# Rows of both moving operands 160 bytes from the weights' place within 256 bytes, where they were 192

## What is computed

```python
hn = rmsnorm(h, norm_mix_g)
proj = hn @ w_in + b_in                       # q, k, v, gates, convolution inputs
y_m = mlstm_and_gate(proj) @ w_branch_m
y_c = (cb * causal_dwconv(cc * ch, conv_w)) @ w_branch_c
h = h + (sigmoid(gm) * y_m + sigmoid(gc) * y_c) @ w_out
hn = rmsnorm(h, norm_ffn_g)
gate, val = split(causal_dwconv(hn @ w_up, ffn_conv_w, ffn_conv_b))
h = h + (silu(gate) * val) @ w_down
```

## The kernel before

| tensor | address before | within 256 | place before |
|---|---|---|---|
| whi, wlo | 49280, 65664 | 128 | |
| hn, from its 64th value, high and low | 98624 + 256 | 64 | 192 |
| act, high and low | 135488 | 64 | 192 |
| hn, from its 48th value (272 columns) | 98624 + 192 | 0 | 128 |
| lo2, row 0, 1, 2, 3 and so on | 208672 + 1088 a row | 32, 96, 160, 224 | 160, 224, 32, 96 |

## Time and profile before

### The profile page before, as it was taken

One profiled execution on the slowest core, in us unless ns is written; L12 is line 12 of the kernel. 1 busy time (PEld: TensorE's weight loads), 2 busy tenths in 40 slices (PEclk: granted clock), 3 DMA queues, 4 the chain that ended last, 5 costly groups with the idle time before them and its releaser, 6 DMA issues.

```text
span 2870.7 us, 53265 instructions
## 1 busy us (share of the span) xinstructions
PE 2744.2 (96%) x22994; PEld 2721.2 (95%) x22994; DVE 1711.4 (60%) x1725; ACT 1300.1 (45%) x1449; POOL 1.8 (0%) x14
## 2 busy tenths in 40 slices
PE   4988999999999999999999967999999999999998
PEld 4987999999999999999989967999999999999998
DVE  4544565566667567657785648755665555455555
ACT  3443454444554355445544375444454334343443
POOL 0000000000000000000000000000000000000000
PEclk9988999999999999999999988999999999999999
DMA  4442555555555555555545424555556565655653
GB/s 154 162 146 93 195 193 192 190 191 191 187 194 180 197 182 196 198 191 165 173 165 171 154 98 132 191 185 182 190 179 189 189 182 187 191 183 185 186 183 115
DMA packets 257814, 503.17 MB, mean 175 GB/s; under 512 B 10150, under 2 KB 19038, under 8 KB 257630
## 3 DMA queue, kind: packets, MB, share of 16 engines
q1 hardware_dynamic: 254592, 500.20, 53.1%
q10 hardware_dynamic: 3054, 0.55, 0.1%
HBM read 498.63 MB, written 2.10 MB: 174 GB/s over the span
## 4 chain that ended last, share of the span: by engine, by line
PE 87%; DVE 7%; ACT 4%; ACTq 1%; issue 1%; DVEq 0%
PE psum L461 27%; PE psum L462 27%; PE psum L463 26%; PE psum L485 2%; PE psum L486 2%; PE psum L487 2%; DVE wlo L1040 2%; DVE work L1068 1%; DVE work L1408 1%; ACT whi L727 1%; ACTq L713 1%; DVE misc L1454 0%; ACT misc L950 0%; DVE hn L1078 0%; DVE work L1439 0%
## 5 line engine op out<-in xcount | busy, mean ns | idle before, releaser
L1040 DVE TENSOR_TENSOR wlo<-raw,whi 128x1024 fp32r<-128x1024 f32 x952 | 1160.1, 1223 | 983.6 <-ACT whi L727 982.7
L727 ACT ACTIVATE whi<-raw 128x1024 fp32r<-128x1024 f32 x952 | 1003.3, 1058 | 1317.4 <-PE psum L463 1194.3
L461 PE MATMUL psum<-hn,whi 128*128 128x256 f32 x4448 | 1249.5, 281 | 38.9 <-DVE wlo L1040 25.9
L462 PE MATMUL psum<-hn,whi 128*128 128x256 f32 x4448 | 1247.0, 280 | 0.0
L463 PE MATMUL psum<-hn,wlo 128*128 128x256 f32 x4448 | 1246.7, 280 | 0.0
L461 PEld LDWEIGHTS psum<-hn,whi 128*128 128x128 f32 x4448 | 846.1, 190 | 42.6 <-DVE wlo L1040 28.9
L463 PEld LDWEIGHTS psum<-hn,wlo 128*128 128x128 f32 x4448 | 848.7, 191 | 0.0
L462 PEld LDWEIGHTS psum<-hn,whi 128*128 128x128 f32 x4448 | 842.5, 189 | 0.1
L461 PE MATMUL psum<-act,whi 128*128 128x256 f32 x2544 | 711.8, 280 | 14.8 <-DVE wlo L1040 9.3
L463 PE MATMUL psum<-act,wlo 128*128 128x256 f32 x2544 | 711.0, 279 | 0.0
L462 PE MATMUL psum<-act,whi 128*128 128x256 f32 x2544 | 710.9, 279 | 0.0
(11 more groups left out here) (207 smaller groups left out, 978.3 us busy)
## 6 DMA issues: line engine op xcount, KB each, us to landing
raw<-in_w_in SPq DMA_DIRECT2D x160, 1024.0 KB, 5.1
raw<-in_mlp_w SPq DMA_DIRECT2D x128, 1024.0 KB, 5.3
raw<-in_w_up SPq DMA_DIRECT2D x80, 1024.0 KB, 5.0
raw<-in_w_down SPq DMA_DIRECT2D x40, 1024.0 KB, 5.1
raw<-in_w_out SPq DMA_DIRECT2D x32, 1024.0 KB, 5.0
raw<-in_w_branch_m SPq DMA_DIRECT2D x8, 1024.0 KB, 5.0
raw<-in_w_branch_c SPq DMA_DIRECT2D x8, 1024.0 KB, 5.0
raw<-in_w_up SPq DMA_DIRECT2D x8, 768.0 KB, 4.4
```

The costliest lines, as they stand in the source:

```text
L461: mm(o, hi[:, kk, w], both[:, 0, :], start=first, stop=False)
L462: mm(o, hi[:, kk, w], both[:, 1, :], start=False, stop=False)
L727: A(whi[:, n % SLOTS, :], raw[:, n // 2 % RAW, n % 2 * HALF:(n % 2 + 1) * HALF], ACT.Copy)\
L1040: V.tensor_tensor(wlo[:, n % SLOTS, :], raw[:, n // 2 % RAW, n % 2 * HALF:(n % 2 + 1) * HALF], whi[:, n % SLOTS, :].bitcast(F32), ALU.subt ...
```

## The change

`gap_a` has 40 values where it had 48. All that is declared behind it lies 32 bytes lower.

```diff
-        sb("gap_a", [P, 48])
+        sb("gap_a", [P, 40])
         hn = sb("hn", [P, NT, MAIN + 2 * T], F32R)
         act = sb("act", [P, NT, 2 * T], F32R)
```

## The result

The changed kernel takes 2931.86 us, the median of four runs (2910.89 to 2938.26), against 2865.29 us before. The ratio on record is 1.022 with a 95% interval from 1.0166 to 1.0273; the quotient of the two medians, 1.023, lies inside it. It is slower by 2.2%, where 2923 us in a range from 2835 to 2942 was forecast. A fifth run, outside the median, took 2922.67 us.

What follows compares the result with a forecast made beforehand. TensorE's distance between matmul starts was taken as the bound. The profiled 2872.45 us plus 51 us for 256-column matmuls, between 38 and 64, with other parts at zero, gave 2923 us, range 2835 to 2942.

Steps and rivals of the forecast that it cites:

- VectorE and ScalarE at other places: Both engines' reads and writes at shifted addresses: priced at zero, with slack as cover.
- Transfers: Transfers into raw, whose address stays: nothing priced.
- The 272-column groups: 1536 matmuls of 272 columns at shifted addresses: at most 2 us either way, taken as nothing.
- The price of place 160: 20976 matmuls of 256 columns, moving rows at 160 instead of 192 bytes (within 256) from the weights: plus 51 us.
- the lower bound: 256-column matmuls: only the 113.35 ns distance is forbidden, all go at 117.7 ns, loss 38 us.
- the middle that was chosen: 256-column matmuls: 51 us, taken between losses of 38 and 64 us.
- the upper bound: 256-column matmuls: 106.7 ns plus the 12.3 ns extra of 272-column matmuls, 119.0 ns, loss 64 us.
- the short pattern: Stretches of 256-column matmuls 113.35 ns apart, 8725 of them before, against 117.7 ns in the others.
- What would show it: Signs: one distance near 118 to 119 ns, none at 113.3, half clock at 213, idle before L461 not growing.
- Only the draw changes: At TensorE's restarts only the pattern fallen into changes; 2868 us, 10 us either way; chance 0.22.
- Place 160 holds the short pattern: Every TensorE restart falls into 113.35 ns; gain 50 us, 2823 us; chance of faster 0.21.
- A dearer place: Rows straddling 64 bytes cost each matmul another 4.4 ns; loss 89 us, 2961 us; chance 0.05.

Runs made afterwards that it cites:

- f2: Against the kernel before, only wlo moved, to 64 bytes (within 256) from the moving rows; whi stays at 192: 2818.87 us, ratio 0.9815.
- place 0: Kernel before with gap_a at 64 values instead of 48, so hn and act lie 0 bytes (within 256) from the weights: 2948.29 us, ratio 1.0280.
- places 64: Kernel before with gap_a at 16 values instead of 48, moving rows 64 bytes (within 256) from the weights: 2892.95 us, ratio 1.0082.
- 96: Kernel before with gap_a at 24 values instead of 48, moving rows 96 bytes (within 256) from the weights: 2947.93 us, ratio 1.0282.
- 224: Kernel before with gap_a at 56 values instead of 48, moving rows 224 bytes (within 256) from the weights: 2914.98 us, ratio 1.0167.
- e1: Changed kernel with 8 values given back behind act, so only hn and act lie 32 bytes lower than before: 2918.61 us, ratio 1.0154.
- e2: Against the kernel before, raw, whi, wlo and h lie 32 bytes higher; hn, act and all behind stay: 2916.82 us, ratio 1.0146.
- e3: Against the kernel before, everything from raw to the last tensor lies 32 bytes higher: 2867.86 us, ratio 0.9992.
- e4: Against the kernel before, hn alone lies 32 bytes lower; act and all behind stay: 2884.40 us, ratio 1.0037.
- f1: Against the kernel before, only wlo moved, to 160 bytes (within 256) from the moving rows; whi stays at 192: 2916.74 us, ratio 1.0159.

## Why the prediction was right

**The reading of what bounds the kernel.** The distance between matmuls was taken as the bound, with two values on one layout. The runs agree. In the profiled executions the mean distance is 113.4 ns in f2, 115.8 before, 118.0 after and 119.9 at place 0, and the time is 2817, 2872, 2911 and 2948 us, with the same instructions on VectorE and ScalarE.

**The parts at zero.** VectorE and ScalarE at other places: the four groups whose tensors moved are within 3 ns of before, and TensorE's wait for weights did not grow. Transfers: their share in the stretches stays at 0.56 to 0.58 in nearly all rows of before and after. The 272-column groups were taken as nothing. A stretch of 74 us inside them holds 590 matmuls in the changed kernel, 125.4 ns, against 589 in the earlier trace rows: nothing as far as can be read. The rows of the changed kernel, of f2 and of place 0:

```profile
1539.00:1613.00 74.00, 74.00 (x590) 1.00 0.50 161
```

```profile
1489.00:1563.00 74.00, 74.00 (x591) 1.00 0.48 160
```

```profile
1560.00:1634.00 74.00, 74.00 (x591) 1.00 0.50 161
```

**The price of place 160.** The bounds were 117.7 and 119.0 ns, for 38 and 64 us. The changed kernel's nine stretches shown above hold 2205 us and 18684 matmuls, 118.0 ns in the mean, in the profiled run; against 115.8 before that is 2.2 ns x 20976 = 46 us, of which 42.5 appear as busy time. The short end of 117.2 lies half a nanosecond under the lower bound and 119.9 one over the upper, so the bounds held for the mean and not for the single stretch. The median went up by 66.6 us, just over the upper 64 and 16 us above the middle that was chosen. The forecast of 2923 us is nevertheless only 9 us below the median, because the sum started from the profiled execution of before, 7 us above the median before; that is luck.

The source of the upper bound does not hold. It carried the 12.3 ns that a matmul of 272 columns takes over its columns to one of 256 columns at place 160. But the rows above give 125.2 ns for 272 columns both in f2, whose 256-column matmuls run at 113.4 ns, and at place 0, where they run at 119.9. The same holds at places 64 (124.4), 96 (125.0) and 224 (124.6), each over 74 us. So the 272-column rows hardly follow the places, and could not price one for 256 columns. That 118.6 and 119.9 ns lie near the 119.0 is luck too. What held up was the other argument, that place 160 forbids the short pattern. It was incomplete: the long one is not kept either, since 117.2, 118.6 and 119.9 ns stand in its place. The middle between the bounds rested on no row. In the traced run the loss by distances is 46 us, under the middle of 51; in the median it is over the upper bound.

**What would show it.** Forecast was one distance of 118 to 119 ns, and no 113.3. The second came true; in place of the one distance there are two in the trace, three over the runs of place 160. Half clock stayed at 213 ns, and the idle time before L461 did not grow (TensorE's waits for weights 32.1 us, 35.3 before).

**The rivals.** *Only the draw changes*: false for 160 (e1, e2), and just what happens when weights and rows move together (e3, 0.9992). *Place 160 holds the short pattern*: false. But its price was right: 50 us or 2823 for all matmuls at 113.35 ns, and f2, which gets there by another way, takes 2818.87. *A dearer place*: 2961 was over anything seen; the dearest places, 0 and 96, take 2948.

**Independent reads.** The Trainium skill, TensorE: Matmul & The Clock Gate (Step-by-step: what each phase is for), says that loading the next weights takes no read bandwidth from the running matmul. If that meant no effect on its time, the runs here would contradict it: with the weights (and `raw` and `h`) 32 bytes higher and the moving rows where they were (e2), the 113.3 ns are gone and stretches of 119.8 ns appear. The measurement decides for the time: the distance between matmuls depends on how the two addresses lie to each other. Whether read bandwidth is the cause, no run shows. The Trainium skill, SBUF — State Buffer (Operand start alignment), says of its alignment rule that it is about legality and that its runs timed nothing; here 32 bytes, with both starts legal for float32, are worth 2%.

**Open.** Why 64 and 192 and not 0; whether 32 or 128 are good; whether `whi` at 64 and `wlo` at 192 do as well as the other way round; why the 272-column matmuls hardly follow the places; what at a restart picks the distance; what a typical run of e4 looks like. No run looked inside the reads, so the mechanism that ties them is not named here.

## What to carry to other kernels

Where weight loads and moving rows stream side by side, read the distance between matmul starts over long stretches: two values on the same instructions were time to be had here, and a spread between runs pointed to them. Then treat the distance between the addresses of weights and moving rows, within 256 bytes, as a parameter, for each kind of weights by itself; here padding alone made 2819 to 2948 us out of the same instructions. Where every row pitch is a multiple of 256 bytes, as for `hn` and `act` here, there is one such distance to choose; what other pitches cost was not tested.

## What the hardware showed that I had not expected

- Two distances, 113.35 and 117.7 ns, on the same addresses, the first held for 489 us and the second for a thousand, and each left only at a restart of TensorE.
- With `whi` at 192 and `wlo` at 64 from the moving rows, the short one is reached after every restart (f2), while one place for both, 192 or 64, gives a mixture.
- The loss of one misplaced load in three (f1, 1.0159) is about that of all three (e1, 1.0154; the change, 1.0220).
- Three of the seven places give one distance all through the run: 119.9 ns at 0 and 96, the dearest, and 118.2 ns at 224.
- At half the granted clock, place 160 costs nothing where it was read: 213.3 ns as at 192. The 272-column matmuls, at full clock, stay within 124.4 to 125.6 ns in the seven kernels read.
